# Blocks of 72 columns for the last eight of fourteen experts, in a loop of their own

## The chip, the cores and the metric

The kernel runs on one core of one Trainium2 chip. The metric is device time in microseconds (us); three runs of the kernel before took 1327.75, 1324.80 and 1324.03 us, median 1324.8 us.

## The reference, cut to what matters

One layer of a hybrid streaming encoder for 1024 prompt frames and 64 sample frames, model width 1024, all float32. Attention and a recurrent mixer come first and are not touched. Then each of the 1088 tokens is routed to two of 32 experts:

```python
def moe(h, lp):
    expert, gate = hier_route(xf, lp)        # 2 experts for each of 1088 tokens
    ...
    def expert_block(args):
        xb, e = args
        return (jax.nn.silu(xb @ lp['w1'][e]) * (xb @ lp['w3'][e])) @ lp['w2'][e]
    ...
    contrib = ys[dest] * g_sorted[:, None]
    return jnp.zeros((t, d), h.dtype).at[tok_sorted].add(contrib)
```

`w1` and `w3` of one expert are 1024 x 512, `w2` is 512 x 1024, 2048 KB each in float32. With the reference's own inputs its router gives the 32 experts, in the order of their numbers, 61 73 77 69 72 66 71 65 68 72 59 71 88 76 68 96 69 49 70 62 50 60 60 58 80 74 71 64 63 53 82 59 rows, 2176 in all.

## The kernel before, in words

After routing, the kernel works through 32 positions, one expert at each. Positions 0 to 2 are experts 0 to 2, whose weights are loaded before routing is known. `sort_experts` (from line 2198) sorts the rest by the number of their rows, largest first, and puts the eight smallest at positions 3 to 10. So the positions hold these numbers of rows: 61 73 77 (positions 0 to 2), 60 60 59 59 58 53 50 49 (3 to 10), 96 88 82 80 76 (11 to 15), 74 72 72 71 71 71 70 69 69 68 68 66 65 64 (16 to 29), 63 62 (30 and 31).

`CAPS` (line 63) gives each position the size of its block: 96 for positions 0 to 2 and 11 to 15, 64 for 3 to 10, 30 and 31, and 80 for 16 to 29. Rows beyond a block's size would go to extra blocks of 96 that run at the end (`over_e`, the branches under `total > 0`); no position has more rows than its block here. An instruction stream can only be unrolled so far, so positions 12 to 15 and 16 to 29 each run in a hardware loop on TensorE (`LOOPS`, line 66), two positions in a pass. A body takes its sizes from the first two positions of its range.

One position, in the order of TensorE's queue (`expert`, from line 1272):

- `hidden_1` (line 1187, 128 matmul records): `w1` of this expert times its rows, into bank 2. The rows are the moving columns of the matmuls: 96 or 80 of them.
- `down` (line 1252, 128 records): `w2` of the expert before, times its hidden values. In an even position of the loop from 16 the column number is that of position 15, so 96; in an odd one it is 80.
- `gather_transposes` (line 1178, 8 records): the next expert's rows, turned.
- `hidden_3` (line 1187 again, 128 records): `w3` of this expert.
- `turn_back` (line 1262, 8 records): the output of the expert before, turned back.

Positions with blocks of 64 use lines 1197, 1228 and 1240 instead.

Weights: SyncE issues every load of 2048 KB (line 614) into two sets of buffers that take turns (three up to position 10, `SETS`). The load of `w1` for position p waits until `hidden_1` of position p-2 is through, and so for `w3` and `w2`.

Rows: GpSimd gathers the rows of position p+4 from `xn_rows` (lines 1767, 1768, 1760) and adds the results to `out_y` by a scatter with accumulation (lines 1786, 1787, 1777). Both take an index for each slot, from the tables `slot_out` and `slot_hi`; an index out of bounds moves nothing. Both go in two transfers from position 11 to 29: slots 0 to 63, and the slots above them. In positions 16 to 29 the second is a transfer of 16 slots, 64 to 79, for the gather and for the scatter. One row is 4 KB. Which row of an expert (its rank) lies in which slot is fixed by a table in `constants()` (line 106): slots below 64 are dealt by `slot % 4 * 16 + slot // 4`, slots 64 to 79 hold ranks 79 down to 64, so that 71 rows fill slots 73 to 79 and leave 64 to 72 empty.

VectorE and ScalarE run positions 12 to 27 in one loop (lines 2411 and following, 1630 and following), at sizes that don't change. GpSimd has loops for positions 12 to 15 and 16 to 27.

Of the kernel before, what the change touches and what calls it, by code (L numbers as in the profile page):

```python
# [28 lines left out]
P = 128  # L29
# [28 lines left out]
TOKENS = SEQ + DEC  # L58
EB = 96
EL = 80  # L60
ET = 64
FIRST = 3
CAPS = [EB] * 3 + [ET] * 8 + [EB] * 5 + [EL] * 14 + [ET] * 2
SETS = [p % 3 for p in range(11)] + [2 * (p % 2) for p in range(11, 30)] + [1, 0]
EARLY, LATE = CAPS.index(ET), len(CAPS) - CAPS[::-1].index(EL)
LOOPS = ((12, 16), (16, 30))
CT = 64
FT = FF // 2
MAX_OVER = 27
# [8 lines left out]
def constants():  # L78

    c = {}  # L80
    c["ident"] = np.eye(P, dtype=np.float32)
    s, t = np.meshgrid(np.arange(P), np.arange(P), indexing="ij")
    c["chunk_mask"] = np.where((s // CH == t // CH) & (s <= t), 0.0, NEG).astype(np.float32)
    c["before"] = (s < t).astype(np.float32)
    pos = np.zeros(ROWS)
    pos[:DEC] = PAST + np.arange(DEC)
    pos[DEC:DEC + META] = np.arange(META) - META
    pos[P:] = np.arange(SEQ)
    half = ROPE // 2
    inv = np.float32(10000.0) ** (-np.arange(half, dtype=np.float32) / np.float32(half))  # L90
    ang = pos.astype(np.float32)[:, None] * inv[None, :].astype(np.float32)
    cos, sin = np.cos(ang).astype(np.float32), np.sin(ang).astype(np.float32)
    table = np.concatenate([cos, cos, -sin, sin], axis=1).reshape(NT, P, 2 * ROPE)
    c["rope"] = np.ascontiguousarray(table.transpose(1, 0, 2).reshape(P, NT * 2 * ROPE))
    keep = np.ones(ROWS, np.float32)
    keep[DEC + META:P] = 0.0
    start = (np.arange(ROWS) % CH == 0)
    rows = [keep[:P], np.where(keep > 0, 0.0, NEG)[:P], np.where(start, 0.0, 1.0), np.where(start, 3 * NEG, 0.0)]
    c["gate_rows"] = np.broadcast_to(np.concatenate(rows).astype(np.float32)[None], (HM, GATE_W)).copy()
    sel = np.zeros((HM, HM, P), np.float32)  # L100
    for h in range(HM):
        sel[h, h] = 1.0
    c["pick_head"] = sel.reshape(HM, HM * P)
    ro = np.zeros((P, ROUTE_W), np.float32)
    slot = np.arange(P)
    ro[:, 0:P] = np.where(slot < ET, slot % 4 * 16 + slot // 4, np.where(slot < EL, ET + EL - 1 - slot, slot))
    ro[:, P:P + NE] = NE - 1 - np.arange(NE)
    ro[:, P + NE:P + 2 * NE] = np.arange(NE)
    at = P + 2 * NE
    ro[:, at:at + NT] = np.arange(NT)[None, :] * P + np.arange(P)[:, None] - NOWHERE  # L110
    ro[DEC:, at + NT] = NOWHERE
    ro[:, at + 2 * NT:at + 2 * NT + FIRST] = 1.0e6 * np.arange(FIRST, 0, -1)
    c["route_rows"] = ro
    return c
# [37 lines left out]
def by_tokens(b):  # L152

    return CAPS[b] == ET

# [16 lines left out]
def gathers_of(p):  # L172

    return 16 * sum(in_parts(q) for q in range(p % 2, p + 1, 2))
# [12 lines left out]
def loads_of(p):  # L187

    return 16 * sum(SETS[q] == SETS[p] for q in range(p + 1))
# [95 lines left out]
def build(nc, T, O):  # L285

    ctx = ExitStack()
    with ctx:
        def sb(name, shape, dt=F32):
            return ctx.enter_context(nc.sbuf_tensor(name, shape, dt))  # L290
# [19 lines left out]
        slot_out = sb("slot_out", [P, NBLK], U32)  # L310
        slot_hi = sb("slot_hi", [EB - ET, NE], U32)
        index_now = sb("index_now", [P, 8], U32)
        now_tok = [index_now[:, i:i + 1] for i in range(2)]
        now_out = [index_now[:, i:i + 1] for i in range(2, 4)]
        hi_tok = [index_now[0:EB - ET, i:i + 1] for i in range(4, 6)]
        hi_out = [index_now[0:EB - ET, i:i + 1] for i in range(6, 8)]
# [555 lines left out]
        def _(pe):  # L872
# [300 lines left out]
            def gather_transposes(s, b, arrived, count, rows):  # L1173

                pe.wait_ge(arrived, count)
                pe.wait_ge(xeT_read, b)
                for k in range(KD):
                    ins = pe.transpose(bank(0, 2)[:, k * P:k * P + rows], xe[s][0:rows, k * P:(k + 1) * P],  # L1178
                                       ident[0:rows, 0:rows])
                ins.then_inc(xeT_full, 1)  # L1180
# [20 lines left out]
            def hidden_1(w, s, b, arrived, count, rows):  # L1201

                pe.wait_ge(arrived, count)
                pe.wait_ge(xeT_read, b + 1)
                pe.wait_ge(u_ok, b)
                ins = up_by_tokens(bank(2), w1s[w], xeT[s]) if rows == ET else up(bank(2), w1s[w], xeT[s], rows)
                ins.then_inc(h1_full, 1)

            def hidden_3(w, s, b, arrived, count, rows):

                halved = isinstance(b, int) and b == NE - 1
                pe.wait_ge(w3_half, 16) if halved else pe.wait_ge(arrived, count)
                pe.wait_ge(xeT_read, b + 1)
                pe.wait_ge(hh_ok, b)
                if rows == ET:
                    ins = up_by_tokens(bank(3), w3s[w], xeT[s], count if halved else None)
                else:
                    ins = up(bank(3), w3s[w], xeT[s], rows)
                ins.then_inc(h3_full, 1)

            def hidden_back(b):

                pe.wait_ge(hh_ok, b + 1)
                pe.wait_ge(y_read, EARLY if b < LATE else LATE)
                if tiled(b) > 1:
                    pe.wait_ge(ht_ok, tiled(b) - 1)
                for i in range(2):
                    ins = pe.transpose(bank(6)[:, i * P:(i + 1) * P], h_row[:, i * P:(i + 1) * P], ident[:])  # L1228
                ins.then_inc(ht_full, 1)
# [14 lines left out]
            def down(w, b, arrived, count, rows):  # L1244

                pe.wait_ge(arrived, count)
                pe.wait_ge(hh_ok, b + 1)
                for j in range(KD):
                    o = bank(4 + j // 4)
                    for k in range(KF):  # L1250
                        for c in range(0, P, CT):
                            ins = pe.matmul(o[c:c + CT, (j % 4) * EB:(j % 4) * EB + rows],  # L1252
                                            w2s[w][:, k, j * P + c:j * P + c + CT], hT[:, k * EB:k * EB + rows],
                                            start=(k == 0), stop=(k == KF - 1))
                ins.then_inc(yT_full, 1)
# [9 lines left out]
            def downs_read(b, q):  # L1265

                if by_tokens(q):
                    pe.wait_ge(y_read, b + 1)
                else:
                    pe.wait_ge(yT_ok, b + 1 - tiled(q))  # L1270

            def expert(p, j=None):

                more, rows_more = (0, 0) if j is None else (16 * j, 32 * j)
                b = p if j is None else p + 2 * j
                s, rows, q = p % 2, CAPS[p], p - 1
                hidden_1(SETS[p], s, b, w1_in[SETS[p]], loads_of(p) + more, rows)
                if by_tokens(q):
                    hidden_back(q)
                    gather_transposes(1 - s, b + 1, xe_in[1 - s], gathers_of(p + 1) + rows_more, CAPS[p + 1]) if p < NE - 1 else None  # L1280
                    downs_read(b - 2, p - 2)
                    down_by_tokens(SETS[q], q, w2_in[SETS[q]], loads_of(q))
                else:
                    if p > 1:
                        downs_read(b - 2, p - 2)
                    down(SETS[q], b - 1, w2_in[SETS[q]], loads_of(q) + more, CAPS[q])
                    gather_transposes(1 - s, b + 1, xe_in[1 - s], gathers_of(p + 1) + rows_more, CAPS[p + 1])
                hidden_3(SETS[p], s, b, w3_in[SETS[p]], loads_of(p) + more, rows)
                if not by_tokens(q):
                    turn_back(b - 1, tiled(q))  # L1290
# [4 lines left out]
            hidden_3(0, 0, 0, w3_in[0], 16, EB)  # L1295
            for p in range(1, LOOPS[0][0]):
                expert(p)
            for lo, hi in LOOPS:
                with pe.Fori(0, (hi - lo) // 2) as j:
# [346 lines left out]
        def _(pool):  # L1646
# [153 lines left out]
            def turn(p, j=None):  # L1800

                b, s, more = (p, p % 2, 0) if j is None else (p + 2 * j, p % 2, 32 * j)
                if p + 4 < NE:
                    e = column(b + 4)
                    pool.wait_ge(xeT_full, b + 3)
                    pool.sem_inc(index_steps, 1)
                    rows = ET if in_parts(p + 4) == 1 else max(EL, CAPS[p + 4])
                    gather(s, b + 4, e, xe_in[s], rows, in_parts(p + 4))
# [12 lines left out]
            pool.wait_ge(hi_ok, 1)  # L1821
            for p in range(0, 12):
                turn(p)
            for lo, hi in ((12, 16), (16, 28)):
                with pool.Fori(0, (hi - lo) // 2) as j:
                    for i in range(2):
                        turn(lo + i, j)
# [679 lines left out]
```

## Time and profile before

| what | us |
|---|---|
| median of three runs | 1324.8 |
| lowest, highest | 1324.03, 1327.75 |
| span of the profiled execution | 1322.7 |
| TensorE busy in it | 1226.0 |
| mean granted TensorE clock | 0.980 |
| data moved by DMA | 278.64 MB |

The profiled execution's own time is given by the page as its span, from the first to the last instruction: 1322.7 us. The median of the runs is 2.1 us more; what lies before and after the span is in the runs and not in the trace. Slices of the page are a fortieth of the span, 33.07 us. Expert work begins at about 765 us.

### The profile page before, as it was taken

How to read it: one execution, taken by the hardware profiler on the slowest of the kernel's cores; microseconds unless marked ns; L12 is line 12 of the kernel's file. 1: busy time of each engine (PE TensorE's matmuls, PEld its weight loads, DVE VectorE, ACT ScalarE, POOL GpSimd, SP SyncE). 2: the span in 40 equal slices, each digit the busy share in tenths (PEclk: the TensorE clock that was granted, in tenths of full speed). 3: DMA queues.
4: the chain of work that ended last, by engine and by line, in shares of the span. 5: the costliest groups of instructions: out<-in, count | busy, mean ns of one | idle time of the engine just before them, and what ended most of it. 6: DMA issues, size and time to landing. Idle time of an engine off the chain costs nothing. (4 is left out here: it accounts for less than half of the span.)

```text
span 1322.7 us, 31681 instructions
## 1 busy us (share of the span) xinstructions
PE 1226.0 (93%) x13264; PEld 868.3 (66%) x13264; DVE 419.6 (32%) x907; ACT 334.8 (25%) x781; POOL 279.3 (21%) x401
## 2 busy tenths in 40 slices
PE   8999999998899999999999879997799899888886
PEld 4554444445565666666666679663699898888883
DVE  2433311025654555554643651111011111111111
ACT  3522110124444545545444100110000000000001
POOL 2220000103312312212111012222122332232321
PEclk9999999999998999999999889998899999999999
DMA  9611211142202202201032979999999999999996
GB/s 344 252 56 40 65 65 41 47 158 68 81 17 66 81 17 66 81 17 59 17 120 105 411 277 368 372 364 373 363 390 369 371 376 376 391 377 378 379 397 232
DMA packets 45276, 278.64 MB, mean 211 GB/s; under 512 B 10280, under 2 KB 15400, under 8 KB 32252
## 3 DMA queue, kind: packets, MB, share of 16 engines
q1 hardware_dynamic: 37088, 254.80, 50.0%
q0 software_dynamic: 6800, 17.84, 5.8%
q10 hardware_dynamic: 1296, 4.72, 1.0%
q8 instruction: 64, 1.05, 0.3%
q14 instruction: 28, 0.23, 0.1%
HBM read 250.49 MB, written 29.83 MB: 212 GB/s over the span
## 5 line engine op out<-in xcount | busy, mean ns | idle before, releaser
L1119 PE MATMUL psum<-arena 128*128 128x512 f32 (+1 forms) x576 | 241.4, 577 | 3.3 <-DVE arena L1878 2.4
L1187 PE MATMUL psum<-arena 128*64 128x80 f32 (+1 forms) x5632 | 224.6, 241 | 14.3 <-DMA arena<-in_w 10.6
L1187 PEld LDWEIGHTS psum<-arena 128*64 128x64 f32 x5632 | 216.6, 139 | 22.6 <-issue 10.9
L1119 PEld LDWEIGHTS psum<-arena 128*128 128x128 f32 x576 | 108.9, 191 | 127.3 <-issue 123.5
L1252 PE MATMUL psum<-arena 128*64 128x96 f32 (+1 forms) x2816 | 115.2, 242 | 23.9 <-issue 15.7
L1252 PEld LDWEIGHTS psum<-arena 128*64 128x64 f32 x2816 | 111.5, 137 | 26.8 <-issue 17.7
L1020 PE MATMUL psum<-arena 128*128 128x512 f32 x288 | 126.9, 593 | 1.8 <-DVE arena L2111 1.0
L1777 POOL DMA_INDIRECT out_y<-arena,index_now x54 | 75.3, 1394 | 178.8 <-ACT arena L1598 112.2
L1658 POOL TENSOR_SCALAR small<-small 128x2 f32<-128x2 f32 (+4 forms) x44 | 10.3, 234 | 448.9 <-DVE small L1859 164.8
L1020 PEld LDWEIGHTS psum<-arena 128*128 128x128 f32 x288 | 53.3, 190 | 63.2 <-issue 61.6
L1598 ACT ACTIVATE arena<-psum,slot_gate 96x1024 f32<-96x1024 f32 x22 | 24.4, 1111 | 277.2 <-PE psum L1262 277.2
L1525 ACT ACTIVATE arena<-psum 16x128 f32<-16x128 f32 (+4 forms) x172 | 57.5, 398 | 128.0 <-PE psum L1075 128.0
L1197 PE MATMUL psum<-arena 128*64 128x256 f32 x640 | 76.9, 396 | 11.3 <-DMA arena<-in_w 11.2
L1063 PE MATMUL psum<-arena 96*128 96x264 f32 (+7 forms) x224 | 77.9, 464 | 3.6 <-ACT arena L1378 3.0
L1197 PEld LDWEIGHTS psum<-arena 128*64 128x64 f32 x640 | 51.2, 143 | 37.3 <-DMA arena<-in_w 15.1
L893 PE MATMUL psum<-ident,arena 128*128 128x128 f32 (+1 forms) x432 | 62.3, 274 | 3.9 <-ACT arena L1493 1.6
L1075 PE MATMUL psum<-ident,arena 128*128 128x128 f32 (+2 forms) x388 | 54.5, 274 | 10.4 <-ACT arena L1505 9.7
L893 PEld LDWEIGHTS psum<-ident,arena 128*128 128x128 f32 (+1 forms) x432 | 48.8, 134 | 20.8 <-issue 14.3
L1505 ACT ACTIVATE arena<-psum,small 128x144 f32<-128x144 f32 (+8 forms) x68 | 51.9, 764 | 37.1 <-DVE small L2094 36.9
L1592 ACT ACTIVATE arena<-psum 128x384 f32<-128x384 f32 (+1 forms) x32 | 14.6, 458 | 182.6 <-PE psum L1187 98.3
L1660 POOL TENSOR_TENSOR small<-small 128x2 f32<-128x2 f32 (+4 forms) x44 | 60.1, 1365 | 3.7
L1075 PEld LDWEIGHTS psum<-ident,arena 128*128 128x128 f32 (+2 forms) x388 | 42.3, 132 | 24.8 <-ACT arena L1505 11.7
(255 smaller groups left out, 1344.6 us busy)
## 6 DMA issues: line engine op xcount, KB each, us to landing
arena<-in_w SPq DMA_DIRECT2D x94, 2048.0 KB, 29.6
z_rows<-arena SPq DMA_DIRECT2D x27, 256.0 KB, 2.0
arena<-z_rows SPq DMA_DIRECT2D x9, 768.0 KB, 5.2
arena<-in_w_in SPq DMA_DIRECT2D x3, 2048.0 KB, 22.6
arena<-in_xT_rows SPq DMA_DIRECT2D x9, 512.0 KB, 10.6
arena<-in_x_rows ACTq DMA_DIRECT2D x9, 512.0 KB, 6.2
arena<-in_x_rows SPq DMA_DIRECT2D x9, 512.0 KB, 6.3
out_y<-arena SPq DMA_DIRECT2D x9, 512.0 KB, 2.6
```

What stands on the lines that cost most here:

```text
L893: ins = pe.transpose(o[0:width, i * P:i * P + rows], src, ident[0:rows, 0:rows])
L1020: ins = pe.matmul(o, mixT[:, k, :], w_out[:, k, lo:lo + BANK], start=(k == 0), stop=(k == KD - 1))
L1063: ins = pe.matmul(o[:, lo:hi], qT[n % 2][:, u, :], KT[:, u, k0 + lo:k0 + hi], start=True, stop=True)
L1075: ins = pe.transpose(o[0:w, i * P:(i + 1) * P], probs[:, lo:lo + w], ident[:])
L1119: ins = pe.matmul(o[:, 0:w], xT[n][:, k, :], w_in[:, at_ + k * w:at_ + (k + 1) * w], start=(k == 0), stop=(k == KD - 1))
L1187: ins = pe.matmul(o[c:c + CT, j * EB:j * EB + rows], w[:, k, j * P + c:j * P + c + CT], x[:, k, 0:rows], start=(k == 0), stop=(k == KD - 1))
L1197: ins = pe.matmul(o[c:c + CT, 0:FT], x[:, k, 0:ET], w[:, k, i * FT:(i + 1) * FT], start=(k == 0), stop=(k == KD - 1))
L1252: ins = pe.matmul(o[c:c + CT, (j % 4) * EB:(j % 4) * EB + rows], w2s[w][:, k, j * P + c:j * P + c + CT], hT[:, k * EB:k * EB + rows], star ...
L1505: act.activation(probs[:, 0:w], bank(0, 3)[:, lo:lo + w], ACT.Exp, bias=nmax[:, u:u + 1], accum_out=rsum[:, u:u + 1]).then_inc(s_read, 1)
L1525: take_pT(lambda d, s: act.activation(d, s, ACT.Copy), o, part, 4 * g, key)
L1660: pool.tensor_tensor(dst, dst, half[:, 0:n], ALU.pow).then_inc(signal, 1)
L1777: pool.indirect_dma_start(O["y"], bass.IndirectOffsetOnAxis(ap=index, axis=0), rows, None, bounds_check=last_token, compute_op=ALU.add, oo ...
```

## The change

A third size, `EM` = 72, is given to positions 22 to 29. TensorE's and GpSimd's loops over positions 16 onward are cut in two at position 22, and the table that deals ranks to slots gets a further case.

```diff
 EL = 80
+EM = 72
 ET = 64
-CAPS = [EB] * 3 + [ET] * 8 + [EB] * 5 + [EL] * 14 + [ET] * 2
+CAPS = [EB] * 3 + [ET] * 8 + [EB] * 5 + [EL] * 6 + [EM] * 8 + [ET] * 2
-EARLY, LATE = CAPS.index(ET), len(CAPS) - CAPS[::-1].index(EL)
-LOOPS = ((12, 16), (16, 30))
+EARLY, LATE = CAPS.index(ET), len(CAPS) - CAPS[::-1].index(EM)
+LOOPS = ((12, 16), (16, 22), (22, 30))
...
-    ro[:, 0:P] = np.where(slot < ET, slot % 4 * 16 + slot // 4, np.where(slot < EL, ET + EL - 1 - slot, slot))
+    ro[:, 0:P] = np.where(slot < ET, slot % 4 * 16 + slot // 4, np.where(slot < EM, ET + EM - 1 - slot, np.where(slot < EL, EM + EL - 1 - slot, slot)))
...
-            for lo, hi in ((12, 16), (16, 28)):
+            for lo, hi in ((12, 16), (16, 22), (22, 28)):
```

With it, slots 64 to 71 hold ranks 71 down to 64, and slots 72 to 79 hold ranks 79 down to 72, for every expert. The second scatter of positions 22 to 29 has 8 slots. Their gathers keep 16, because line 1807 takes `max(EL, CAPS[p + 4])`.

## Rows read from the trace of the kernel before

**Rows 1.** The page, in 40 slices: TensorE, its clock, DMA share, bandwidth.

```profile
PE   8999999998899999999999879997799899888886
PEclk9999999999998999999999889998899999999999
DMA  9611211142202202201032979999999999999996
GB/s 344 252 56 40 65 65 41 47 158 68 81 17 66 81 17 66 81 17 59 17 120 105 411 277 368 372 364 373 363 390 369 371 376 376 391 377 378 379 397 232
```

**Rows 2.** The chain of waits in order of time: start us, length us, what.

```profile
1144.89 5.52 PE psum L1252 x128
...
1150.58 29.58 DMA arena<-in_w
...
1180.20 5.52 PE psum L1252 x128
...
1185.89 30.07 DMA arena<-in_w
...
1216.01 5.52 PE psum L1252 x128
...
1262.87 38.99 DMA arena<-in_w
```

**Rows 3.** TensorE's timeline, positions 22 and 23: start, length, line, shape, [idle before].

```profile
1138.57 4.65 PE L1187 MATMUL psum<-arena 128*64 128x80 f32 x128
1144.89 5.50 PE L1252 MATMUL psum<-arena 128*64 128x96 f32 x128 [1.67 <-DMA arena<-in_w]
1150.32 0.77 PE L1178 MATMUL psum<-ident,arena 80*128 80x80 f32 x8
1151.02 4.65 PE L1187 MATMUL psum<-arena 128*64 128x80 f32 x128
1155.60 1.08 PE L1262 MATMUL psum<-ident,arena 128*96 128x128 f32 x8
1156.61 4.65 PE L1187 MATMUL psum<-arena 128*64 128x80 f32 x128
1162.43 4.65 PE L1252 MATMUL psum<-arena 128*64 128x80 f32 x128 [1.17 <-issue]
```

**Rows 4.** TensorE's waits in 1138 to 1281 us: in total, times, longest.

```profile
PE psum L1252 <- DMA arena<-in_w: 6.4, 4, 1.7
PE psum L1252 <- issue: 5.8, 4, 1.8
PE psum L1187 <- DMA arena<-in_w: 2.2, 4, 0.6
```

**Rows 5.** TensorE's timeline at the first pass of the loop from 16.

```profile
1038.83 3.68 PE L1252 MATMUL psum<-arena 128*64 128x96 f32 x82 [1.62 <-issue]
1044.85 3.40 PE L1187 MATMUL psum<-arena 128*64 128x80 f32 x92 [0.24 <-issue]
1051.12 3.69 PE L1187 MATMUL psum<-arena 128*64 128x80 f32 x101 [0.75 <-issue]
1058.41 3.81 PE L1252 MATMUL psum<-arena 128*64 128x80 f32 x102 [2.65 <-issue]
1064.63 4.09 PE L1187 MATMUL psum<-arena 128*64 128x80 f32 x112 [1.00 <-issue]
```

**Rows 6.** DMA in 1138 to 1281 us, slices of 3.6 us, queues, time to landing.

```profile
DMA  9999999999999999999999999999999999999999
q1 hardware_dynamic: 3452, 50.25, 88.5%
q0 software_dynamic: 1792, 4.41, 12.9%
arena<-in_w SPq DMA_DIRECT2D x24, 2048.0 KB, 30.5
```

**Rows 7.** DMA share in 1290 to 1318 us, slices of 0.7 us.

```profile
DMA  9999899999989999999976555433229592000000
```

**Rows 8.** DMA share in 765 to 790 us, slices of 0.625 us.

```profile
DMA  5753926999997954100009669999999998999999
```

## The prediction

> **What bounds the kernel now.** I read the page's slices first. From the 25th slice on (794 us) DMA stands at 9 tenths and moves 360 to 400 GB/s, while TensorE is at 8 or 9 tenths [rows 1]: both look full, so the order of waits must decide. The chain of waits does: over positions 18 to 29 it alternates between one `down` of 5.5 us and about 30 us of weight loads, and the last such piece is 38.99 us long [rows 2]. The timeline says the same from TensorE's side. In a position of the loop it works 15 to 16 us and then stands before `down` for 1.67 or 1.17 us, short of `w2` [rows 3]. Summed over positions 22 to 29 the waits are 6.4 + 5.8 + 2.2 = 14.4 us [rows 4]. I count the 5.8 us that are put down to "issue" as late loads too, since they stand at the same instruction of every second position. So from position 18 or so the stage is paced by the weight loads, 35.3 us for two positions (1144.89 to 1180.20 us [rows 2]), and a load takes 30.5 us from issue to landing [rows 6] where its share of 35.3 us for six loads is 5.9: some five are always queued. A faster TensorE issues the next load earlier into a queue that is full anyway.
>
> The third thing I looked for is whether the 16 DMA engines carry equal work, because a load is only there when its slowest engine is through. The views don't name engines, but they show their spread. When the loads ran dry at 773 us the share fell from 9 to nothing in four or five slices of 0.625 us [rows 8], about 3 us. At the end, where no further load is queued, it falls from 9 at 1304 us through 7, 6, 5, 4, 3 to 2 at 1310 us [rows 7], and the last `w2` half is still awaited around 1311 us. Some engines are done six to ten us before others. The end of the kernel is that of the engine that is last.
>
> **The change part by part.**
>
> Fewer columns on TensorE. A group of 128 records costs 5.50 us at 96 columns and 4.65 at 80 [rows 3], 0.053 us a column, so 72 give 4.22. In an even position of the new loop `hidden_1` and `hidden_3` lose 0.43 each and `down` goes from 96 to the 80 of position 21, 0.85 less: 1.71. In an odd one all three lose 0.43: 1.28. Four pairs make 12.0 us, and position 30's `down` of position 29 makes 12.4. All of it lies beside loads that pace the stage; it becomes more waiting in the places of rows 4, and I count it at 0. If loads did not pace it, it would be worth up to 12.4 us.
>
> The new loop on TensorE. The trace shows what the first pass of a loop costs: at position 16 TensorE stands 1.62 + 0.24 + 0.75 + 2.65 + 1.00 = 6.26 us with nothing to wait for [rows 5]. The same again at positions 22 and 23. Cover: a quarter of the 14.4 us of waits, 3.6, and the 3.0 that the pair's columns save, 6.6 us in all. Loads issued late by some us go to engines with five loads before them. So 0; without that cover, 6.3.
>
> GpSimd's new loop: its two positions stay far from the path (gathers are issued four positions ahead). One body more at a first pass, with TensorE's 6.3 us as the bound: 0 taken. ScalarE and VectorE have the same instructions except for one smaller VectorE operation at position 28: 0.
>
> The extra blocks: positions 22 to 29 have 70 rows at most, below 72, so none is made, and the same 4 KB rows are moved. The scatters drop 8 slots each, but empty ones, which move nothing: 0 bytes.
>
> Which engine moves which row. This is the step on which my forecast rests. With 16 upper slots an engine has one slot, if a transfer is cut into equal shares in the order of its slots; that is my assumption, for no view names engines. Before, a position with 71 rows fills slots 73 to 79, so engines 9 to 15; after, slots 65 to 71, so engines 1 to 7. Counted for positions 3 to 31 with the row numbers and tables of the code, gather and scatter each one row: before, engines 0 to 7 move 246 to 248 rows and engines 8 to 15 move 242 to 246. The table before happens to put the upper rows of positions 16 to 29 on the engines that positions 3 to 15 had left with fewer (by position 15: 118 to 120 for engines 0 to 7, falling to 92 for 12 to 15). After, positions 16 to 21 give engines 1 to 5 twelve rows more each, 6 and 7 ten more, 0 six more; positions 22 to 29 add the gathers (7 to engine 7, 6 to 6, 5 to 5 and 4, 3 to 3, 1 to 2) and scatters of 8 slots, whose engines the trace doesn't show: between none and all of these numbers again, and I take half; small shifts in positions 11 to 15 come on top (4 more for engines 0 and 1, 4 fewer for 4 and 5). Sum: engines 1 to 5 move 14 to 17 rows more, 6 and 7 move 19 to 21 more, 0 moves 10 more, and the engines from 8 on 6 to 21 fewer. The spread goes from 6 rows to about 47.
>
> The price of a row: in 1138 to 1281 us the row queue held 12.9% of 16 engines for 143 us, 295 us, for 4.41 MB or 1077 rows of 4 KB: 0.274 us a row [rows 6]. Lower bound: the peak slice of the stage, 397 GB/s [rows 1], is 24.8 GB/s an engine, 0.165 us a row. Upper bound: a scatter with accumulation may cost twice a gather with that same mean, so 0.365 for it. The last engine gets 16 to 20 rows more: 4.4 to 5.5 us, and I take 4.8. Its queue is never empty, so nothing hides it: a load lands later by that much, TensorE waits for it. At the bounds, 16 rows at 0.165 make 2.6 and 21 at 0.365 make 7.7.
>
> Here the Trainium skill speaks against a change that shortens blocks. Its page "DMA: Bandwidth & Descriptors", section "Why a DMA increments its semaphore by 16 and not by 1", says that a transfer is shared over the largest number of engines up to 16 that divides its outer dimension, and that on GpSimd's queue a number below 16 means consecutive engines from a cursor that moves on. By that rule 16 slots go to 16 engines, as I assume, and 8 slots to one half of the engines at a time, alternately; that would give the half that I take. No row here shows it. The same page ("Latency and other measured facts") says that engines 7 and 15 are usually slower; were 7 the last one, its 20 rows would make it 5.5 us.
>
> **Sum.** The span of the profiled execution is 1322.7 us; plus 4.8 it is 1327.5. The median of the runs lies 2.1 us above the span, and I keep that: 1329.6 us.
>
> **The rivals.**
>
> Nothing moves: 1324.8 to 1325.5 us. Either the engines' rows don't matter because an engine's time is not additive, or slots are dealt in turn (slot i to engine i mod 16). For 16 slots that is the same, but then the big and small positions load other engines: counted this way the fullest engine had 268 rows before (14) and has 270 after (6), 0.5 us. For it: the spread in rows before would be 50 rows, 13.7 us, not far from the six to ten seen [rows 7], while my sharing explains only 1.6 us with rows; the rest must be a difference between the engines themselves. Against it: nothing in the views.
>
> Faster, with the last engine in the upper half. As rows leave over six us of the spread unexplained, the engine that is last may be one of 12 to 15 for a reason of its own. It then loses 20 rows, 5.5 us, while the lower half gains 4 to 5; the time falls by what the lower half was ahead, less its own gain. With the six to ten us of spread, 3 us: 1321.8. It decides when the last engine led the lower half by more than 5 us. Against it: the upper half had 28 rows fewer by position 15, so it should be ahead.
>
> Faster, TensorE paces after all: 12.4 less, 1312.4 us. Rows 4 stand against it.
>
> Slower, the loop's first pass reaches the path: 6.3 us more in place of or beside the rows, 1331 to 1336. For it: the cover of 6.6 is thin. Against it: at positions 16 and 17 the same stall left DMA at 9 throughout [rows 1], and the loads had 30 us in hand.
>
> **How the numbers follow.** Forecast (rows pile up on the late engines) 0.60; nothing moves 0.24; last engine in the upper half 0.06; TensorE paces 0.03; the first pass on the path 0.07. About 0.3%, 4.0 us, is what can be told from no change. The forecast's own range is 2.6 to 7.7 us more, 1327.4 to 1332.5, and about seven tenths of it lie beyond 4.0: 0.43. With the first pass slower holds 0.50; same is 0.17 + 0.24 = 0.41; faster 0.09. The range of 8 in 10 takes in "nothing moves" and the top of the forecast: 1323.5 to 1333.5.
>
> **What would show it.** In the changed kernel: (a) line 1187 at 72 columns at 4.2 us, and `down` at 4.65 and 4.2; (b) TensorE's waits in positions 22 to 29 grow from 14.4 us by more than the 12.4 saved, to 30 or so; (c) DMA still 9 throughout, with the same MB; (d) at the end the share starts to fall earlier (some 5 us before 1304) and ends later, over 15 us and more; (e) 6 us of "issue" at the first pass from position 22. The forecast is wrong if the pairs from 1144 us on keep 35.3 us and the tail of the DMA share keeps its length, or if waits shrink.

## The result: 0.6% slower, and the profile after

The changed kernel takes 1334.25 us in the median of four runs (1330.07, 1332.77, 1335.73, 1353.02) against 1324.41 us; ratio 1.0058, 95% interval 1.0038 to 1.0079, which is 7.7 us. The run of 1353.02 us counts as a slow one and is left out of the ratio; the median of the other three is 1332.77 us. The profiled execution has a span of 1333.9 us where the one before had 1322.7. Lines of the kernel are one higher than before.

The page after, the lines that answer to [rows 1] and the queue that carries instructions (packets, MB, share of 16 engines):

```profile
PE   8999999998999999999998799987899899886897
PEclk9999999999898999999999789999899999997999
DMA  9611210141201201201124989999999999999996
GB/s 351 245 50 40 72 61 36 46 175 50 81 17 65 81 32 50 81 17 58 59 77 176 359 325 368 362 351 376 382 368 377 370 370 372 376 384 365 337 380 222
q8 instruction: 79, 1.29, 0.4%
```

The same queue on the page before:

```profile
q8 instruction: 64, 1.05, 0.3%
```

Two things to see: in the fourth slice from the end the clock digit has fallen to 7, where before it stayed at 9, and 15 more packets of instructions came, 16 KB each. One body of TensorE's loop is 1621 instructions of 64 bytes in the compiled program (800 matmuls and as many weight loads among them), 103.7 KB or 6.3 packets, so the new body explains six or seven of the 15. The DMA view of two stretches, 1138 to 1190 us (the new body's first pass) and 1190 to 1270 us, shows where they all are:

```profile
q8 instruction: 6, 0.10, 0.7%
q8 instruction: 9, 0.15, 0.7%
```

The kernel before has no instruction packet in 1138 to 1281 us.

TensorE's timeline after, the lines with idle time from the first pass of the new loop on; the rows that answer to [rows 3]:

```profile
1142.50 4.22 PE L1188 MATMUL psum<-arena 128*64 128x72 f32 x128
1149.05 0.35 PE L1253 MATMUL psum<-arena 128*64 128x80 f32 x3 [2.33 <-DMA arena<-in_w]
1149.81 6.09 PE L1253 MATMUL psum<-arena 128*64 128x80 f32 x125 [0.41 <-issue]
...
1161.91 0.47 PE L1188 MATMUL psum<-arena 128*64 128x72 f32 x7 [1.41 <-issue]
...
1170.14 1.24 PE L1188 MATMUL psum<-arena 128*64 128x72 f32 x17 [3.10 <-issue]
...
1176.74 0.78 PE L1253 MATMUL psum<-arena 128*64 128x72 f32 x17 [0.80 <-issue]
...
1182.96 1.09 PE L1188 MATMUL psum<-arena 128*64 128x72 f32 x27 [1.47 <-issue]
...
1206.42 5.86 PE L1253 MATMUL psum<-arena 128*64 128x72 f32 x128 [2.82 <-issue]
...
1223.59 0.51 PE L1188 MATMUL psum<-arena 128*64 128x72 f32 x4 [5.49 <-issue]
1228.99 6.91 PE L1188 MATMUL psum<-arena 128*64 128x72 f32 x124 [4.90 <-issue]
...
1241.59 0.59 PE L1179 MATMUL psum<-ident,arena 72*128 72x72 f32 x6 [0.99 <-issue]
...
1249.00 0.75 PE L1188 MATMUL psum<-arena 128*64 128x72 f32 x7 [2.86 <-issue]
...
1266.35 1.09 PE L1188 MATMUL psum<-arena 128*64 128x72 f32 x27 [2.29 <-issue]
```

The first pass (positions 22 and 23) stalls 7.2 us in the manner of [rows 5]. The second runs without such stalls inside a group; the 2.82 us at 1206 us stand before a `down`, where the kernel before waits too. But at 1218 us, when the third pass begins, TensorE stands 5.49 and 4.90 us around four records, and the stalls go on to 1266 us: 16.5 us in a body that had run twice. The nine packets fall in this third pass. Its waits in 1138 to 1281 us, answering to [rows 4]:

```profile
PE psum L1188 <- issue: 21.5, 7, 5.5
PE psum L1253 <- issue: 4.0, 3, 2.8
PE psum L1253 <- DMA arena<-in_w: 2.3, 1, 2.3
PE psum L1179 <- issue: 1.0, 1, 1.0
```

28.8 us against 14.4, but only 2.3 are put down to weights and 2.8 more stand before a `down`; the other 23.7 are the stalls inside groups. And DMA in 1215 to 1262 us, slices of 1.2 us, is no longer full:

```profile
DMA  9999989999999887759779997799959789999997
```

Starts of `gather_transposes` of some positions, read off the timelines, in us from that of position 0 (single executions; differences under 2 us say little):

| kernel | 21 | 23 | 24 | 26 | 27 | 28 | 31 |
|---|---|---|---|---|---|---|---|
| before | 347.8 | 383.5 | 400.2 | 436.1 | 454.7 | 471.7 | 523.9 |
| after | 351.3 | 388.2 | 409.8 | 444.5 | 472.6 | 492.3 | 536.7 |

Up to 23 the changed kernel is 4 to 5 us behind; after its first pass about 10; at 27 and 28 it is 18 to 21 behind, and by 31 it has won back 8 us.

So there was a rival that I had only as "the first pass": a body fetched again. Theory R is the prediction's (rows on the late DMA engine), F is the fetch of instructions.

### The profile page after: what moved, and what is told of

It reads as the page before. It is cut to its first block and busy times, and to the rows that moved or that the text cites. A ratio compares the mean times of both kernels' runs of the same rounds, so it can differ in the third digit from the quotient of the medians.

```text
span 1333.9 us, 31685 instructions
## 1 busy us (share of the span) xinstructions
PE 1224.4 (92%) x13264; PEld 867.3 (65%) x13264; DVE 420.1 (31%) x909; ACT 334.7 (25%) x781; POOL 280.1 (21%) x401
## 2 busy tenths in 40 slices
DMA packets 45293, 278.89 MB, mean 209 GB/s; under 512 B 10281, under 2 KB 15401, under 8 KB 32253
## 5 line engine op out<-in xcount | busy, mean ns | idle before, releaser
L1188 PE MATMUL psum<-arena 128*64 128x96 f32 (+2 forms) x5632 | 221.0, 240 | 32.7 <-issue 25.4
L1253 PE MATMUL psum<-arena 128*64 128x96 f32 (+2 forms) x2816 | 117.4, 247 | 18.7 <-issue 11.5
L2360 DVE SCALAR_TENSOR_TENSOR arena<-arena,psum 128x384 f32<-128x384 f32 (+1 forms) x32 | 16.3, 509 | 139.7 <-ACT arena L1593 139.7
```

The source lines that it names most:

```text
L1188: ins = pe.matmul(o[c:c + CT, j * EB:j * EB + rows], w[:, k, j * P + c:j * P + c + CT], x[:, k, 0:rows], start=(k == 0), stop=(k == KD - 1))
```

## The experiments

Each was timed in five rounds beside the kernel before; "ratio" is to it, with its interval.

**e1, the new table alone.** Blocks of 80, loops as before.

```diff
-np.where(slot < EL, ET + EL - 1 - slot, slot))
+np.where(slot < 72, ET + 72 - 1 - slot, np.where(slot < EL, 72 + EL - 1 - slot, slot)))
```

> The kernel before with only the new table of ranks: all blocks and loops as before. Theory R (rows pile up on the late DMA engines): slower by 4 to 6.6 us (24 rows more on the fullest engine at 0.274 us), the last weight loads land that much later, TensorE's waits in positions 22 to 29 grow from 14.4 us by the same amount, and no more instruction packets (64) than before. Theory F (the cost is TensorE's instruction fetch in the new loop): no change, within 2 us.

Measured: 1328.22 us, ratio 1.0036 (1.0020 to 1.0051), 64 instruction packets. The table alone costs 4.8 us. Its timeline at the `down` of positions 26 and 28, and its waits in 1138 to 1281 us:

```profile
1217.72 5.50 PE L1252 MATMUL psum<-arena 128*64 128x96 f32 x128 [1.38 <-DMA arena<-in_w]
...
1253.88 5.50 PE L1252 MATMUL psum<-arena 128*64 128x96 f32 x128 [1.57 <-DMA arena<-in_w]
```

```profile
PE psum L1252 <- issue: 7.3, 4, 1.9
PE psum L1252 <- DMA arena<-in_w: 6.3, 4, 1.7
PE psum L1187 <- DMA arena<-in_w: 3.5, 6, 1.0
```

The pair takes 36.2 us where the kernel before takes 35.5 (1216.01 us in [rows 2] to its next at 1251.52), and TensorE's waits grow from 14.4 [rows 4] to 17.1, those for `w1` and `w3` among them from 2.2 to 3.5. Counted from position 0, position 21 starts 1.0 us later than in the kernel before, 24 starts 2.8 later and 28 starts 4.0 later (single executions): the delay builds up where loads pace the stage. Theory R holds in kind: same bytes, same instructions, another order of rows, a slower load. No view names the engine; that it is rows per engine and not some other effect of the order of rows is what the next two runs ask.

**e10, upper ranks in ascending order.** In place of the table's reversal: `slot`.

> The kernel before with ranks 64 to 79 in slots 64 to 79 in ascending order, nothing else. By equal shares in order of slots engine 0 moves 30 rows more, 1 moves 28, 2 and 3 22, 4 18, 5 14, 6 6, 7 none, and 8 to 15 fewer; in the run with the new table alone it was 10 for engine 0 rising to 24 for 7. Theory R with the late engine at 0 to 3: slower than the new table alone, 6 to 9 us above before. Theory R with the late engine at 6 or 7 and the others a few us ahead: less than the new table alone, 0 to 4 us above before. Engine rows without effect: no change.

Measured: 1327.49 us, ratio 1.0018 (1.0003 to 1.0033): 2.4 us, less than the new table, though engines 0 to 3 get more rows by the count, 4 as many, and only 5, 6 and 7 get fewer. Late engines at 6 or 7 would make that. The intervals of e1 and e10 overlap, so it is an indication. The Trainium skill ("DMA: Bandwidth & Descriptors", section "Latency and other measured facts") says that engines 7 and 15 are usually slower than the others; e10 does not speak against it, and no view here shows an engine by itself.

**e3, the deal of slots 0 to 63 turned by eight engines.**

```diff
-slot % 4 * 16 + slot // 4
+slot % 4 * 16 + (slot // 4 + 8) % 16
```

> The kernel before with the deal of slots 0 to 63 turned by eight engines (slot // 4 + 8 modulo 16): by the count engines 0 to 7 move 0 to 12 rows fewer in positions 3 to 10 and engines 8 to 15 as many more. Theory R: engines of the lower half are last, so 1 to 3 us faster, and the DMA share falls more steeply at the end. Theory F: no change. If the late engine is in the upper half: 1 to 3 us slower.

Measured: 1325.42 us, ratio 1.0001 (0.9990 to 1.0013). A miss: 10 rows taken off engines 5 to 7 in positions 3 to 10 should have given 2 us and gave nothing. Either loads don't pace those positions, so that engines level out there, or the 64 slots are not shared as I counted. The prediction's first rival has another sharing, slot i to engine i mod 16. By it the turn by eight moves no row to another engine, since slots i, i+16, i+32 and i+48 only exchange their ranks, so it forecasts just what e3 measured. Counted that way for e1 and e10, engine 7 still gets 24 and 4 rows more than before. So e3 speaks for this sharing and against the one that the forecast used.

The kept traces hold something that no view prints: a weight load reports its end in 16 parts, as many as there are DMA engines, and each part has its time. From the first to the last part it took, in us, as the mean of the loads that ended in each stretch (seven to nine loads):

| kernel | 1050 to 1100 | 1100 to 1150 | 1150 to 1200 | 1200 to 1250 | 1250 to 1320 |
|---|---|---|---|---|---|
| before | 16.8 | 16.0 | 14.2 | 12.6 | 11.6 |
| e1 | 17.2 | 18.0 | 19.4 | 20.7 | 21.4 |
| e3 | 16.8 | 15.8 | 13.8 | 13.0 | 12.0 |
| changed kernel | 17.4 | 18.9 | 21.0 | 18.4 | 9.1 |

In the kernel before the parts draw together as the upper rows of positions 16 to 29 come, as the prediction had it for its engines; with the new table they drift apart, by 9.8 us more at the end, and with e3's deal nothing changes. By either sharing e1 gives engine 7 24 rows more and engine 15 24 fewer, so my estimate is 9.8 / 48 = 0.20 us a row.

**e2, the loops cut and nothing else.** Blocks of 80, old table.

```diff
-LOOPS = ((12, 16), (16, 30))
+LOOPS = ((12, 16), (16, 22), (22, 30))
...
-            for lo, hi in ((12, 16), (16, 28)):
+            for lo, hi in ((12, 16), (16, 22), (22, 28)):
```

> The kernel before with only the loops of TensorE and GpSimd cut at position 22: blocks of 80 and the old table. Theory R: no change, the 6.3 us of a first pass are covered by waits, within 2 us. Theory F: 5 to 10 us slower, with stalls of several us in later passes of the loop from 22 and more than 70 instruction packets where before has 64.

Measured: 1340.94 us (1331.96 to 1353.19), ratio 1.0122 (1.0079 to 1.0164), 79 instruction packets. Cutting the loops costs 16 us by the ratio (10 to 22), but its runs differ: 1331.96, 1332.26, 1335.01, 1346.88, 1348.36, 1353.19. The lower three lie where three runs of the changed kernel lie, and its fourth, 1353.02, lies where the upper three do. Its profile, of the run of 1331.96, has the same picture as the changed kernel's, 5.86 and 5.22 us at the start of the third pass. Theory R had said "no change"; F is right here.

**e4, two loops again.** The changed kernel with positions 12 to 21 in one loop of TensorE at 96 columns: `LOOPS = ((12, 22), (22, 30))`.

> The changed kernel with TensorE's positions 12 to 15 and 16 to 21 in one loop at 96 columns, so that there are two loops as in the kernel before; GpSimd's loops, the blocks of 72 and the new table stay. Theory F with the number of loop bodies as its cause: back to 1 to 5 us above before, instruction packets near 64 and no stall in a later pass. Theory R alone: as the changed kernel without its stalls, 4 to 6 us above before. If the stalls come with the passes of the loop from 22 whatever stands before it: 8 to 11 us above before.

Measured: 1328.94 us, ratio 1.0029 (1.0015 to 1.0043), 64 packets, no stall in a later pass. Either the number of bodies matters or where the last one lies: in this kernel it lies where the body from 16 lies before. The next runs move code without changing work. The places where a first pass stalls show where a packet ends. The changed kernel's third body first stalls after 131 pairs of weight load and matmul, 262 instructions, and a packet is 256, so the packet edge before that one lies a few instructions after the body's start, and 0.97 + 6.33 = 7.30 reaches into an eighth packet. By such places the bodies from 12 and 16 lie over seven packets, and the third one of the changed kernel (starting at 0.97 of a packet) over eight.

**e5, e6, e7, the code shifted.** Waits on `tab_ok` that are already met, ahead of the first gather: 51 instructions in the kernel before (e5), 97 in the changed kernel (e6) and in e2's (e7). Two waits make one instruction, so the edit has 102 of them in e5 and 194 in e6 and e7.

```diff
             pe.wait_ge(tab_ok, 1)
+            for _ in range(102):
+                pe.wait_ge(tab_ok, 1)
```

> The kernel before with 51 more instructions (waits that are already met) in TensorE's program, placed where it waits for the first gather anyway, 762 us. Instructions come in packets of 16 KB (64 packets, 1.05 MB, in the kernel before); a loop body of TensorE is 1621 instructions of 64 bytes, 6.3 packets, and counted from the places where the first pass stalls, the bodies from 12 and from 16 lie over 7 packets each. The shift puts the body from 16 over 8. Theory F8 (a body over 8 packets is fetched again in later passes): 10 to 30 us slower, more than 75 instruction packets, stalls in the passes from 1070 us on. Theory Fn (the third loop as such is the cause, wherever its code lies): no change, within 2 us. Theory R: no change.

> The changed kernel with 97 such instructions, after which all three bodies lie over 7 packets (before the shift the one from 22 lies over 8). Theory F8: the stalls of later passes go, instruction packets 70 (64 and one body), and what is left is the rows on the late engine: 3 to 5 us above the kernel before. Theory Fn: as the changed kernel, 8 to 11 us above before.

> Only the loops cut, blocks of 80 and the old table, with the same 97 instructions, all bodies over 7 packets. Theory F8 with R: nothing is left, within 2 us of the kernel before, the first pass of the new body under the waits for weights. Theory Fn: as the cut loops without the shift, 15 us slower. If a first pass alone costs time: 2 to 6 us slower.

Measured: e5 1358.66 us, ratio 1.0250 (1.0225 to 1.0274), 91 packets. 51 idle instructions, run while TensorE waits for something else, cost the kernel before 33 us. Its timeline, stalls at the start of every second pass:

```profile
1115.05 1.85 PE L1189 MATMUL psum<-arena 128*64 128x80 f32 x22 [6.31 <-issue]
...
1196.57 1.86 PE L1189 MATMUL psum<-arena 128*64 128x80 f32 x22 [6.99 <-issue]
...
1276.19 1.85 PE L1189 MATMUL psum<-arena 128*64 128x80 f32 x22 [6.59 <-issue]
```

But e6 is at 1350.31 us (ratio 1.0191, 1.0172 to 1.0209) with 89 packets and e7 at 1353.91 (1.0216, 1.0197 to 1.0236) with 88: I had expected them cured. The timeline of e6 says which body it is:

```profile
1093.39 6.77 PE L1190 MATMUL psum<-arena 128*64 128x80 f32 x128 [13.05 <-issue]
...
1141.53 6.60 PE L1190 MATMUL psum<-arena 128*64 128x80 f32 x128 [10.70 <-issue]
```

It is the body from 16, whose passes begin at 1093 and 1142 us; the one from 22 has no stall after its first pass. By the place of its first stall the shift of 97 had set the start of the body from 16 one instruction ahead of a packet's edge: eight packets. So the third body was cured and the second broken; the shift was miscounted by an instruction or two. That is for theory F8 (a body over eight packets is fetched again in later passes), but it could also be that any shift costs.

**e8, e9, all three bodies over seven packets,** 80 instructions ahead of all loops and 30 between the first two; e8 from the changed kernel, e9 from e2's.

> The changed kernel with 80 more instructions of TensorE ahead of the loops and 30 between the loops from 12 and from 16. The last shift of 97 put the start of the body from 16 one instruction short of a packet's edge, by the place of its first stall, and that body was fetched again in every pass; the one from 22 was not. Now the bodies start at 0.59, 0.05 and 0.40 of a packet, so each lies over 7. Theory F8: no body is fetched again, instruction packets 70, what is left is the rows: 3 to 5 us above the kernel before. Theory Fn (a third loop is the cause) or theory Fs (any shift of the code costs): 15 to 30 us above before.

> Only the loops cut at 22 (blocks of 80, old table), with the same 80 and 30 instructions. Theory F8 with R: within 2 us of the kernel before, 70 instruction packets. Theories Fn or Fs: 15 to 30 us above before.

Measured: 71 packets in both and no second fetch, as F8 has it. F8 had 3 to 5 us for e8 and under 2 us for e9, the others 15 to 30, and the times lie between: e8 1335.12 us, 1.0077 (1.0052 to 1.0102); e9 1331.34, 1.0054 (1.0036 to 1.0071). The first pass of the body from 16 took longer than before (24 us from the transposes of position 16 to those of 17, for 19.1), and their profiled executions have short stalls of 0.3 to 0.45 us in every position after GpSimd's transfers. e10's execution has these too at the code layout of before, so they come from something else than the shift; what, stays open. Code shifted ahead of the loops thus came with some 7 us in e9 that no run here explains, without any second fetch.

**e11, e12, only the third body moved.** 20 instructions between the loops from 16 and from 22, so that everything ahead lies as before; e11 from the changed kernel, e12 from e2's.

```diff
             for lo, hi in LOOPS:
+                if lo == 22:
+                    for _ in range(40):
+                        pe.wait_ge(tab_ok, 1)
```

> The changed kernel with 20 more instructions of TensorE between the loops from 16 and from 22, so that only the third body moves: it starts at 0.04 of a packet and lies over 7, where it lay over 8; everything ahead of it lies as in the kernel before. Theory F8: no second fetch of the body (71 instruction packets, not 79), no jump of 8 to 10 us at position 27; left are the rows (3 to 5 us) and part of the first pass, 4 to 8 us above the kernel before and 2 to 5 below the changed kernel. If the second fetch has another cause: as the changed kernel, 8 to 11 us above before.

> Only the loops cut at 22 (blocks of 80, old table) with the same 20 instructions ahead of the third body. Theory F8: 71 packets, and only the third body's first pass is left, 0 to 4 us above the kernel before, where the cut loops without the shift were 15 us above. If the second fetch has another cause: 8 to 20 us above before.

Measured: e12 1326.54 us, ratio 0.9999 (0.9978 to 1.0020); e11 1330.84 us, ratio 1.0036 (1.0017 to 1.0055); 70 packets in both. The third pass of e11, where the changed kernel stands for 16.5 us:

```profile
1212.73 4.22 PE L1188 MATMUL psum<-arena 128*64 128x72 f32 x128
1216.88 1.08 PE L1263 MATMUL psum<-ident,arena 128*96 128x128 f32 x8
1217.89 4.22 PE L1188 MATMUL psum<-arena 128*64 128x72 f32 x128
1224.36 5.87 PE L1253 MATMUL psum<-arena 128*64 128x80 f32 x116 [2.25 <-DMA arena<-in_w]
```

No second fetch, and a wait for weights again. With the seven packets, and everything ahead of the third body left in place, the cut of the loops costs nothing that these runs can tell, and what the change then costs is what e1's table alone costs.

| kernel | blocks | table | third body over | ratio | packets |
|---|---|---|---|---|---|
| e12 | 80 | old | 7 | 0.9999 | 70 |
| e1 | 80 | new | none | 1.0036 | 64 |
| e4 | 72 | new | none | 1.0029 | 64 |
| e11 | 72 | new | 7 | 1.0036 | 70 |
| changed kernel | 72 | new | 8 | 1.0058 | 79 |
| e2 | 80 | old | 8 | 1.0122 | 79 |
| e9 (code ahead shifted) | 80 | old | 7 | 1.0054 | 71 |
| e8 (code ahead shifted) | 72 | new | 7 | 1.0077 | 71 |

e9 and e8 have no second fetch and are still 7 and 5 us above e12 and e11. No version beat the kernel before: where TensorE's columns are fewer the loads still set the pace, and e12, its equal, only has more code.

## Why the prediction was right in one half and wrong in the other

**What bounds the stage.** Right. 12.4 us less matmul gave nothing in e4 and e11, which are slower than the kernel before, and e11 with 72 columns costs what e1 costs with 80.

**Columns at 0.** Right: 128 records take 4.22 us at 72 columns, as worked out, and they buy nothing while loads pace the stage. Whether they are worth something in the changed kernel as it is, where fetches hold TensorE back, is not shown. By the ratios the second fetch costs about 16 us with 80 columns (e2 less e12) and 2.9 with 72 (changed kernel less e11), but these 2.9 leave out the run of 1353.02 us, and the intervals of the changed kernel and e11 overlap. In the two profiled executions the difference is small: e2, with 80 columns, is 15.4 us behind the kernel before at position 28 and 9.4 at 31, so it wins back 6 us where the changed kernel wins back 8. Most of that recovery is not the columns: after its stand TensorE finds the weights there and works without waiting until the loads pace it again.

**Rows on the late engines, 4.8 us.** The step that carried the forecast. e1 and e11 both measure 1.0036, 4.8 us, with 2.7 to 6.8 us as e1's interval. In e1 all scatters have 16 slots, so the count for engine 7 is 24 rows rather than 20, and the price of a row comes to 0.2 us, 0.11 to 0.28 by the interval, where the prediction took 0.274. The spread of the loads' parts gives 0.20 too. So more rows at a lower price made the 4.8 us in e1, and that the changed kernel's own 20 rows came to the forecast's figure to the tenth is in part luck: e11's interval is 2.3 to 7.3 us. The engine itself was not seen, and e3 is against the way in which the prediction shares 64 slots over the engines. So what is shown is that the table makes the loads late and makes their 16 parts end further apart, as unequal rows would; that the late engine is one of 6 and 7 is argued.

**The new loop at 0.** The step that failed, in this form: I took the cost of a loop from its first pass and no more. The first pass is indeed covered, as I had it: 7.2 us of stalls, and e12 at 0.9999, 2.7 us at most by its interval. The cover takes a few positions to work: e12 is 7.7 us behind at position 24 and 1.9 at 27. What I left out is that a body can be fetched again in a later pass, since in the kernel before none is: both its bodies lie over seven packets, and the last instruction of the body from 16 is, by the places of its first stalls, 0.05 of a packet short of an eighth. My rival "the loop's first pass reaches the path" named the right engine with the wrong mechanism, and gave 1331 to 1336.

**The sum.** 1329.6 us was forecast, with a range of 1323.5 to 1333.5. The ratio puts the changed kernel at 1332.1, and the median of the three runs that it uses is 1332.77, both inside; the median of all four, 1334.25, is 0.75 above. Of the 7.7 us by the ratio 4.8 are the table's; the 2.9 left are the second fetch less whatever was won back, a term that the prediction had not. So the changed kernel lies near the top of the range partly for a reason that the range was not made for. The forecast's own mechanism is best compared with e11, at 1330.84 us.

**The signs.** (a) held. (b) The waits doubled as forecast, 28.8 us, but for the wrong reason: 23.7 of them are stalls inside groups and 5.1 waits before a `down`, and only the view by instruction shows that. (c) failed: DMA fell to 5 and 7 in slices after 1230 us, and the page has 278.89 MB, 0.25 more than before, which is the 15 packets. (d) failed, and the likely cause is the same: in 1215 to 1262 us a load took 18.0 us from issue to landing where it had taken 30.5, so fewer were queued, and the loads' 16 parts, 21.0 us apart before the stand, are 9.1 apart after it: the engines drew level. In e1, with the rows alone, the share (1290 to 1318 us, slices of 0.7 us) dips first at 1301 us and falls from 1305 as steeply as in [rows 7], although its last loads' parts end 21.4 us apart and not 11.6. The share is a mean over 16 engines and hides this:

```profile
DMA  9989999989999998889997655432210008960000
```

(e) held.

A page of the Trainium skill bears on the failed step: "Runtime: NRT & Kernel Launch", section "Instruction fetch mechanics". It says that TensorE holds 128 KiB of instructions, filled in blocks of 16 KiB, and that a taken branch to a target outside the current window of two pages makes the engine wait for a fetch. The trace agrees on the block (1.05 MB in 64 packets). On the window it does not: by two pages every pass of a body of 6.3 packets would be fetched, and the kernel before fetches none of its passes after the first. Eight blocks are 128 KiB. That a body over eight does not stay, while one over seven does, fits all the runs: e2, e5, e6, e7 and the changed kernel have such a body and fetch it again, e8, e9, e11 and e12 have none and don't. That filling one block ahead is what pushes the first one out is my reading, not shown.

## What to carry to other kernels

Fewer columns on an engine that waits for loads give nothing; look at what else the edit moves, and here that was a table of slots, worth 0.36% by itself and, by the count, a matter of how evenly 16 DMA engines were loaded. Every edit that adds or removes instructions ahead of a large hardware loop shifts its code: count the blocks that the body lies over, and compare the instruction packets on the page before and after. A kernel that is level or tight in such a thing by luck or by hand (the table of ranks, the 0.05 of a block) shows nothing of it in its own profile.

## What was not expected of the hardware

- 51 instructions that do nothing, ahead of a loop of 1621, made the kernel 33 us slower (e5), with 27 more packets of instructions of 16 KB. A shift of 80 without a second fetch cost e9 7 us, so not all of the 33 need be the fetches.
- A body over eight packets is fetched again in every second pass (e5: at 1115, 1197 and 1276 us; changed kernel: third of four), one that starts an instruction ahead of a packet's edge in every pass, 11 to 13 us each (e6). A second fetch in the changed kernel is nine packets. Why these differ was not tried.
- The clock falls too. While TensorE stands 5.49 and 4.90 us in the third pass, the granted clock falls from 1.00, the level of 2.4 GHz, to 0.50, the level of 1.2 GHz, in 1222 to 1234 us, and is back at 1.00 in 1236 to 1248; the 124 records at 1229 us take 6.91 us where 128 take 4.22 at full clock. Over 1210 to 1245 us it is 0.79 with TensorE busy for 23.62 us of 35, where the kernel before has 1.00. Columns (us, TensorE busy, weight loads busy, VectorE, ScalarE, GpSimd, clock, DMA share, GB/s):

```profile
1222.00:1234.00 12.00, 5.52 (x89) 5.42 (x91) 0.00 (x0) 0.00 (x0) 1.37 (x1) 0.50 0.95 361
1210.00:1245.00 35.00, 23.62 (x556) 22.73 (x554) 4.85 (x6) 1.60 (x2) 6.80 (x12) 0.79 0.96 363
```

- Executions of e2 differ by 21 us among themselves (1331.96 to 1353.19) where those of the kernel before differ by 7, so the cost of a second fetch varies; only the lowest of them has a profile, and what the upper three do is not known.
